# Seven block products in two units of five of a streamed fp32 down projection

## The chip, the core and the metric

One core of a Trainium2 chip runs the whole program. The metric is the time of one execution on the device in microseconds (us), as the median of several runs. Engines are named as the profile names them: PE (TensorE's matmuls), PEld (its weight loads), DVE (VectorE), ACT (ScalarE), POOL (GpSimd) and SP (the DMA queue that streams the weights).

## The reference

One layer of a hybrid block for 256 tokens and a model width of 2048, all in float32: a mixing part (gated MLP and windowed attention), then a gated MLP with a convolution of width 3. The change touches only the last matrix product.

```
def conv_ffn(h, w_up, conv_w, w_down):      # h (256, 2048), w_up (2048, 16384), w_down (8192, 2048)
    up = h @ w_up
    ...
    gate, val = conv[..., :D_FF], conv[..., D_FF:]
    return (jax.nn.gelu(gate, approximate=True) * val) @ w_down
...
x = x + rms_norm(conv_ffn(h2, w_up, conv_w, w_down), ln_post_ffn)
```

## The kernel before

**Splitting.** PE multiplies fp32r operands. To keep float32 accuracy each operand is held as a rounded part ("hi", written by ACT as a copy into an fp32r tile) and the rest ("lo", written by DVE as full minus hi), and each product is made as hi*hi + hi*lo + lo*hi, three matmuls. So every weight that comes from memory passes through ACT, then DVE, before PE may use it.

**The down projection.** `ffT` holds the 8192 hidden values of 256 tokens, transposed: 64 tiles of 128 hidden values by 256 tokens. Two sweeps each make 1024 of the 2048 output columns. A sweep reads the weights in 32 units of 1 MB (2 tiles of 128 hidden rows by 1024 columns) into the four slots of `raw`. A unit is two halves, each 128 hidden rows by 1024 columns. An ordinary half goes through a ring of four places in `w_hi`, `w_lo` and `xs`, and costs PE 2 token tiles x 3 parts x 2 column blocks = 12 matmuls of 512 columns (`half_b`, L1528); a unit costs 24.

**Units of seven products.** A unit is also a 2 x 2 by 2 x 2 block product: two tiles of hidden values, two tiles of 128 tokens, two blocks of 512 columns. For one unit in three of a sweep's middle the kernel makes it from seven block products instead of eight (Strassen's scheme in Winograd's form): 7 x 3 = 21 matmuls (`seven_products`, L1782 is the matmul's line). Its operands are not in the ring but in one set of buffers, the "forms": `b_hi`, `b_lo`, `s_hi`, `s_lo` (all inside `actT`) and `a_hi`, `a_lo` (`a_parts`). There is one set, so it must not be overwritten before PE has finished the seven products that read it. For such a unit ACT and DVE do this:

- `sum_forms` (DVE): seven sums and differences of the weight and activation blocks, in float32.
- `round_given` (ACT) and `rest_of_given` (DVE): hi and lo of the blocks that are used as they are.
- `round_sums` (ACT) and `rest_of_sums` (DVE): hi and lo of the sums.

Four of the seven products accumulate in four extra banks of PSUM; after the last such unit of a sweep `copy_p1` and `sum_products` make the terms that these banks still owe to the outputs, and in sweep 1 `round_u`, `rest_of_u` and `add_products` add them back with eight matmuls by an identity matrix.

**Counters.** Each engine runs its own list of instructions in order, and a wait holds all that stands behind it on that engine. `half_used` counts the halves that PE has finished since the kernel's start (a unit of seven products adds 2 at its end); `N_DOWN` is its value when the down projection begins. `hi_ready` and `lo_ready` count halves on ACT and DVE in the same numbering, `form_hi`, `form_lo` and `form_summed` count steps on the forms. `before` is the value of `half_used` at which all units ahead of a given place are done: before the change that place is the start of a group of three units, of which the third has the seven products. The wait in front of the first instruction that writes the forms is this one, in `round_given`:

```
act.wait_ge(half_used, gr.before - (4 if gr.first else 0))
```

SP refills a slot of `raw` when `lo_ready` says that DVE has read its unit.

Of the kernel before, what the change touches and what calls it, by code (L numbers as in the profile page):

```python
# [18 lines left out]
ALU = mybir.AluOpType  # L19
ACT = mybir.ActivationFunctionType  # L20
AX = mybir.AxisListType
F32 = mybir.dt.float32
# [52 lines left out]
def block_program(nc, x, x_t, pre_gains, w_in, ln_v_g, ln_v_b, w_spatial, b_spatial, rel_bias, sinks, w_a_out, w_b_out,  # L75
# [10 lines left out]
    with ExitStack() as ctx:  # L86
# [89 lines left out]

        def part_of_actT(k):
            return actT[:, k:k + 2, :, :].rearrange("p k a s -> p (k a s)")
# [240 lines left out]
        def _(act):  # L419
# [315 lines left out]
            def round_given(gr):  # L735

                block = raw[:, gr.slots[2], :]
                act.wait_ge(raw_landed[gr.slots[2]], gr.landed[2])
                act.wait_ge(half_used, gr.before - (4 if gr.first else 0))
                act.activation(b_hi[:, B2:BT], block[:, 2 * BLK:4 * BLK], ACT.Copy).then_inc(form_hi, 1)  # L740
                act.activation(b_hi[:, B1:B2], block[:, 0:BLK], ACT.Copy).then_inc(form_hi, 1)
                act.activation(a_hi[:, 0:S], ffT[:, gr.k + 5, :], ACT.Copy).then_inc(form_hi, 1)
                act.activation(a_hi[:, S:S + P], ffT[:, gr.k + 4, 0:P], ACT.Copy).then_inc(form_hi, 1)

            def round_sums(sweep, gr):

                n = SUMS * gr.forms
# [3 lines left out]
                act.activation(s_hi[:, 0:3 * P], s123, ACT.Copy).then_inc(form_hi, 1)  # L751
# [4 lines left out]
            def down_group(sweep, gr):  # L756

                for j in range(4):
                    if gr.first and j == 2:
                        round_given(gr)  # L760
                    act.wait_ge(half_used, gr.freed + j)
                    act.activation(xs[:, j, 0, :], ffT[:, gr.k + j, :], ACT.Copy)  # L762
                    slot = gr.slots[j // 2]
                    act.wait_ge(raw_landed[slot], gr.landed[j // 2])
                    act.activation(w_hi[:, j, :], raw[:, slot, j % 2 * HALF:(j % 2 + 1) * HALF], ACT.Copy).then_inc(hi_ready, 1)  # L765
                if not gr.first:
                    round_given(gr)
                round_sums(sweep, gr)

            def copy_p1(sweep, used):  # L770

                act.wait_ge(half_used, used)
                act.activation(yn[sweep][:, 0, 0:BLK], ps[:, 4 * sweep, :], ACT.Copy).then_inc(u_copied, 1)
# [8 lines left out]
            def down_turn(sweep, i, first=False, last=False):  # L782
# [3 lines left out]
                for h in range(LEFT if last and sweep == 0 else 0, 8):  # L786
                    if first and sweep == 1 and h == 2:
                        copy_p1(0, 8 * m - 2)
                    if first and sweep == 1 and h < 2:
                        free = h - 7  # L790
                    elif first and sweep == 1 and h < RING:
                        free = h - 3
                    elif last and sweep == 0:
                        free = h - 3
                    elif last and h < RING:
                        free = FREED[h]
                    else:
                        free = None
                    split_xs(m, h, ffT[:, 8 * i + h, :], free=free)
# [7 lines left out]
                    if last and sweep == 1 and h == 3:  # L807
                        copy_p1(1, 8 * m)
                        round_u()
# [5 lines left out]
            for sweep in range(2):  # L815
# [3 lines left out]
                for g in range(GROUPS[sweep]):  # L819
                    down_group(sweep, Group(sweep, g))  # L820
# [12 lines left out]
        def _(dve):  # L833
# [465 lines left out]
            def sum_forms(sweep, gr):  # L1299

                n = SUMS * gr.forms
                block = raw[:, gr.slots[2], :]
# [3 lines left out]
                a11, a21 = ffT[:, gr.k + 4, 0:P], ffT[:, gr.k + 4, P:S]  # L1306
                a12, a22 = ffT[:, gr.k + 5, 0:P], ffT[:, gr.k + 5, P:S]
# [15 lines left out]
            def rest(lo, full, hi):  # L1323
                dve.tensor_tensor(lo, full, hi.bitcast(F32), ALU.subtract).then_inc(form_lo, 1)

            def rest_of_given(gr):

                n = HALVES_HI * gr.forms
# [528 lines left out]
```

## Time and profile before

| | |
|---|---|
| median of 3 runs | 1600.2 us (1600.09 to 1600.46) |
| the profiled execution: its own time | 1600.68 us |
| the profiled execution: span of its instructions | 1598.9 us |
| mean granted TensorE clock | 0.999 of full speed |
| PE busy | 1589.9 us (99%) |
| DVE busy, whole span | 1221.4 us (76%) |
| ACT busy, whole span | 821.1 us (51%) |
| units of seven products | 17 (9 in sweep 0, 8 in sweep 1) |

The time of an execution is its span and a little around it: 1600.68 - 1598.9 = 1.8 us here. Busy times of PE are modelled, since matmuls overlap: a matmul's row says how long it is under way, and what it costs in a dense stream is the distance from its start to the next one's start.

### The profile page before, as it was taken

How to read it: one execution, taken by the hardware profiler on the slowest of the kernel's cores; microseconds unless marked ns; L12 is line 12 of the kernel's file. 1: busy time of each engine (PE TensorE's matmuls, PEld its weight loads, DVE VectorE, ACT ScalarE, POOL GpSimd, SP SyncE). 2: the span in 40 equal slices, each digit the busy share in tenths (PEclk: the TensorE clock that was granted, in tenths of full speed). 3: DMA queues.
4: the chain of work that ended last, by engine and by line, in shares of the span. 5: the costliest groups of instructions: out<-in, count | busy, mean ns of one | idle time of the engine just before them, and what ended most of it. 6: DMA issues, size and time to landing. Idle time of an engine off the chain costs nothing.

```text
span 1598.9 us, 24334 instructions
## 1 busy us (share of the span) xinstructions
PE 1589.9 (99%) x8673; PEld 1377.3 (86%) x8673; DVE 1221.4 (76%) x1777; ACT 821.1 (51%) x1119; POOL 2.0 (0%) x12
## 2 busy tenths in 40 slices
PE   9999999999999999999999999999999999999998
PEld 8888888888888888888888888888888888888886
DVE  6556677677766787777777777777777899979996
ACT  6544544456555654444444444444444656566663
POOL 0000000000000000000000000000000000000000
PEclk9999999999999999999999999999999999999999
DMA  9885455546565465656556565565655565546552
GB/s 369 268 230 185 159 184 171 171 158 210 193 255 193 149 210 184 192 184 200 185 184 190 185 200 186 184 189 185 200 186 184 210 232 190 210 160 235 203 192 79
DMA packets 234947, 313.17 MB, mean 196 GB/s; under 512 B 5360, under 2 KB 209808, under 8 KB 234000
## 3 DMA queue, kind: packets, MB, share of 16 engines
q1 hardware_dynamic: 231056, 306.44, 58.2%
q10 hardware_dynamic: 3840, 6.05, 1.5%
q8 instruction: 33, 0.54, 0.1%
q14 instruction: 18, 0.15, 0.0%
HBM read 309.58 MB, written 2.88 MB: 195 GB/s over the span
## 4 chain that ended last, share of the span: by engine, by line
PE 99%; DVE 0%; ACT 0%; issue 0%; DVEq 0%
PE ps L1445 44%; PE ps L1449 23%; PE ps L1536 20%; PE ps L1782 5%; PE ps L1584 3%; PE ps L1549 1%; PE ps L1460 1%; PE ps L1465 0%; PE ps L1673 0%; PE ps L1654 0%; PE ps L1606 0%; PE ps L1666 0%; PE ps L1683 0%; PE ps L1731 0%; DVE arena L1421 0%; PE ps L1489 0%
## 5 line engine op out<-in xcount | busy, mean ns | idle before, releaser
L837 DVE TENSOR_TENSOR w_lo<-raw,w_hi 128x1024 fp32r<-128x1024 f32 x464 | 557.4, 1222 | 243.3 <-ACT w_hi L428 240.4
L428 ACT ACTIVATE w_hi<-raw 128x1024 fp32r<-128x1024 f32 x462 | 478.0, 1057 | 513.3 <-PE ps L1445 261.1
L1445 PE MATMUL ps<-actT,w_hi 128*128 128x512 f32 x3072 | 717.1, 390 | 0.0
L1445 PEld LDWEIGHTS ps<-actT,w_hi 128*128 128x128 f32 x3072 | 569.9, 188 | 114.1 <-issue 0.2
L1449 PEld LDWEIGHTS ps<-actT,w_lo 128*128 128x128 f32 x3072 | 383.4, 191 | 10.0 <-issue 1.7
L1449 PE MATMUL ps<-actT,w_lo 128*128 128x256 f32 x3072 | 389.4, 283 | 0.0
L1536 PE MATMUL ps<-w_hi,xs 128*128 128x512 f32 x944 | 255.4, 389 | 0.0
L1536 PEld LDWEIGHTS ps<-w_hi,xs 128*128 128x128 f32 x944 | 177.2, 188 | 36.7
L1536 PE MATMUL ps<-w_lo,xs 128*128 128x512 f32 x472 | 145.3, 389 | 0.0
L1249 DVE SCALAR_TENSOR_TENSOR arena<-arena,convw 128x256 f32<-128x256 f32 x256 | 106.8, 480 | 0.1
L1536 PEld LDWEIGHTS ps<-w_lo,xs 128*128 128x128 f32 x472 | 88.6, 188 | 18.4
L1359 DVE TENSOR_TENSOR w_lo<-raw,w_hi 128x1024 fp32r<-128x1024 f32 x68 | 83.4, 1226 | 0.0
L848 DVE TENSOR_TENSOR arena<-ps,arena 128x512 f32<-128x512 f32 (+1 forms) x106 | 72.6, 685 | 1.6 <-ACT arena L441 1.6
L765 ACT ACTIVATE w_hi<-raw 128x1024 fp32r<-128x1024 f32 x68 | 71.2, 1047 | 0.0
L441 ACT ACTIVATE arena<-ps 128x512 f32<-128x512 f32 x106 | 61.4, 580 | 2.9 <-PE ps L1465 1.4
L1782 PE MATMUL ps<-actT 128*128 128x512 f32 x204 | 57.7, 391 | 0.0
L843 DVE TENSOR_TENSOR xs<-arena,xs 128x256 fp32r<-128x256 f32 x58 | 24.6, 423 | 43.1 <-ACT w_hi L428 42.8
L434 ACT ACTIVATE xs<-arena 128x256 fp32r<-128x256 f32 x58 | 24.0, 414 | 61.9 <-PE ps L1536 50.8
L762 ACT ACTIVATE xs<-arena 128x256 fp32r<-128x256 f32 x68 | 27.9, 410 | 43.4 <-PE ps L1536 43.4
L1237 DVE TENSOR_TENSOR arena<-arena,rrow 128x512 f32<-128x512 f32 x64 | 44.3, 693 | 6.5
L1782 PE MATMUL ps<-actT,a_parts 128*128 128x512 f32 x153 | 46.7, 395 | 0.0
L1245 DVE TENSOR_SCALAR arena<-arena,convw 128x256 f32<-128x256 f32 x128 | 39.5, 351 | 8.9 <-DVE arena L1237 0.2
(176 smaller groups left out, 881.4 us busy)
## 6 DMA issues: line engine op xcount, KB each, us to landing
raw<-in_w_up_dram SPq DMA_DIRECT2D x128, 1024.0 KB, 5.8
raw<-in_w_down_dram SPq DMA_DIRECT2D x64, 1024.0 KB, 5.2
raw<-in_w_in_dram SPq DMA_DIRECT2D x58, 1024.0 KB, 5.2
raw<-in_w_o_dram SPq DMA_DIRECT2D x16, 1024.0 KB, 5.2
raw<-in_w_a_out_dram SPq DMA_DIRECT2D x8, 1024.0 KB, 5.5
raw<-in_w_b_out_dram SPq DMA_DIRECT2D x8, 1024.0 KB, 5.5
arena<-in_x_dram SPq DMA_DIRECT2D x1, 2048.0 KB, 17.1
arena<-in_x_dram ACTq DMA_DIRECT2D x2, 1024.0 KB, 6.6
```

Of the source, the lines that this page charges most:

```text
L428: act.activation(w_hi[:, h % RING, :], raw[:, h // 2, h % 2 * HALF:(h % 2 + 1) * HALF], ACT.Copy)\
L441: act.activation(lo_part, ps[:, bank:bank + 2, S:2 * S], ACT.Copy).then_inc(copied, 1)
L765: act.activation(w_hi[:, j, :], raw[:, slot, j % 2 * HALF:(j % 2 + 1) * HALF], ACT.Copy).then_inc(hi_ready, 1)
L837: dve.tensor_tensor(w_lo[:, h % RING, :], raw[:, h // 2, h % 2 * HALF:(h % 2 + 1) * HALF], w_hi[:, h % RING, :].bitcast(F32), ALU.subtract ...
L848: dve.tensor_tensor(dst, ps[:, bank:bank + 2, 0:S], lo_part, ALU.add).then_inc(summed, 1)
L1249: dve.scalar_tensor_tensor(out=dst[:, a, :], in0=src[:, a, i:i + S], scalar=w(i, a), in1=dst[:, a, :], op0=ALU.mult, op1=ALU.add).then_inc ...
L1359: dve.tensor_tensor(w_lo[:, j, :], raw[:, gr.slots[j // 2], j % 2 * HALF:(j % 2 + 1) * HALF], w_hi[:, j, :].bitcast(F32), ALU.subtract).th ...
L1445: return pe.matmul(ps[:, bank + c, :], w_hi[:, h % RING, at:at + P], actT[:, k, :, :].rearrange("p a s -> p (a s)"), start=start, stop=stop)
L1449: return pe.matmul(ps[:, bank + c, 0:S], w_lo[:, h % RING, at:at + P], actT[:, k, 0, :], start=start, stop=stop)
L1536: ins = pe.matmul(ps[:, bank + 2 * t + c, :], xpart[:, tokens], wpart[:, slot, c * 512:(c + 1) * 512], start=(first and xpart is x_hi and ...
L1584: ins = pe.matmul(ps[:, 4 + 2 * t + c, :], xpart[:, t * P:(t + 1) * P], wpart[:, slot, c * 512:(c + 1) * 512], start=(k == 0 and xpart is ...
L1782: ins = pe.matmul(ps[:, bank, :], x[x_part], y[y_part], start=(first and alone and x_part + y_part == 0), stop=(last and alone and x_part ...
```

## The change

In a sweep's middle 25 units now form five groups of five, and the third and the fifth unit of each (`s1`, `s2`) have seven products: 20 in both sweeps instead of 17. The two token tiles change places in the scheme, so that the given activation blocks lie side by side and one instruction (128x384) converts them where there were two (128x256 and 128x128). PE waits three times at such a unit: for the given blocks (`form_lo` + 3), for the sums' first part (`form_lo` + 5), and for all (`lo_ready`). A class `Unit` takes the place of `Group`: its `before` belongs to the unit itself. Three units (halves 2 to 7 of the last turn) are left at a sweep's end, and the work of `copy_p1`, `sum_products`, `round_u`, `rest_of_u` and `add_products` is placed between those halves.

```diff
-        SUMS, HALVES_HI = 7, 7
-        FREED = (-5, -4, -3, -2)
-        GROUPS = ((FF // P // 2 - RAW) // 3, (FF // P // 2 - 2 * RAW) // 3)
-        LEFT = (RAW + 3 * GROUPS[0]) * 2 - (FF // P - 8)
-
-        class Group:
-
-
-            def __init__(self, sweep, g):
-                unit = RAW + 3 * g
-                self.k = 2 * unit
-                self.before = N_DOWN + FF // P * sweep + 2 * unit
-                self.freed = self.before - (3 if g == 0 else 5)
-                self.slots = [(unit + x) % RAW for x in range(3)]
-                self.landed = [16 * ((self.before // 2 + x) // RAW + 1) for x in range(3)]
-                self.forms = GROUPS[0] * sweep + g
-                self.first = g == 0
+        SUMS, HALVES_HI = 7, 5
+        GROUPS = 5
+        SEVENS = [RAW + 5 * g + x for g in range(GROUPS) for x in (2, 4)]
+        LEFT = 2 * (RAW + 5 * GROUPS) - (FF // P - 8)
+        DONE = [N_DOWN + FF // P * sweep + 2 * u + j + 1
+                for sweep in range(2) for u in range(FF // P // 2) if u not in SEVENS for j in range(2)]
+
+        class Unit:
+
+
+            def __init__(self, sweep, u):
+                self.k = 2 * u
+                self.before = N_DOWN + FF // P * sweep + 2 * u
+                self.slot = u % RAW
+                self.landed = 16 * (self.before // 2 // RAW + 1)
+                sevens = [x for x in SEVENS if x < u]
+                self.forms = len(SEVENS) * sweep + len(sevens)
+                self.place = (FF // P - 2 * len(SEVENS)) * sweep + 2 * (u - len(sevens))
+                self.first = u == SEVENS[0]
+                self.last = u == SEVENS[-1]
+
+        SEVENS_DONE = [Unit(sweep, SEVENS[-1]).before + 2 for sweep in range(2)]
+
+        def free_at(sweep, h):
+
+            place = Unit(sweep, h // 2).place + h % 2
+            return DONE[place - RING] if place >= RING else N_DOWN + place - RING + 1
...
-            def round_given(gr):
-
-                block = raw[:, gr.slots[2], :]
-                act.wait_ge(raw_landed[gr.slots[2]], gr.landed[2])
-                act.wait_ge(half_used, gr.before - (4 if gr.first else 0))
+            def round_given(unit):
+
+                block = raw[:, unit.slot, :]
+                act.wait_ge(raw_landed[unit.slot], unit.landed)
+                act.wait_ge(half_used, unit.before - (4 if unit.first else 0))
                 act.activation(b_hi[:, B2:BT], block[:, 2 * BLK:4 * BLK], ACT.Copy).then_inc(form_hi, 1)
                 act.activation(b_hi[:, B1:B2], block[:, 0:BLK], ACT.Copy).then_inc(form_hi, 1)
-                act.activation(a_hi[:, 0:S], ffT[:, gr.k + 5, :], ACT.Copy).then_inc(form_hi, 1)
-                act.activation(a_hi[:, S:S + P], ffT[:, gr.k + 4, 0:P], ACT.Copy).then_inc(form_hi, 1)
-
-            def round_sums(sweep, gr):
-
-                n = SUMS * gr.forms
+                act.activation(a_hi, given(unit), ACT.Copy).then_inc(form_hi, 1)
+
+            def round_sums(sweep, unit):
+
+                n = SUMS * unit.forms
                 act.wait_ge(form_summed, n + 2)
                 act.activation(b_hi[:, BT:BT + 2 * BLK], yn[sweep][:, 0, :], ACT.Copy).then_inc(form_hi, 1)
                 act.wait_ge(form_summed, n + 6)
-                act.activation(s_hi[:, 0:3 * P], s123, ACT.Copy).then_inc(form_hi, 1)
+                act.activation(s_hi[:, 0:3 * P], s123, ACT.Copy)
                 act.activation(s_hi[:, 3 * P:4 * P], s4, ACT.Copy).then_inc(form_hi, 1)
                 act.wait_ge(form_summed, n + 7)
                 act.activation(b_hi[:, BT + 2 * BLK:BT + 4 * BLK], yn[sweep][:, 1, :], ACT.Copy).then_inc(hi_ready, 2)
 
-            def down_group(sweep, gr):
-
-                for j in range(4):
-                    if gr.first and j == 2:
-                        round_given(gr)
-                    act.wait_ge(half_used, gr.freed + j)
-                    act.activation(xs[:, j, 0, :], ffT[:, gr.k + j, :], ACT.Copy)
-                    slot = gr.slots[j // 2]
-                    act.wait_ge(raw_landed[slot], gr.landed[j // 2])
-                    act.activation(w_hi[:, j, :], raw[:, slot, j % 2 * HALF:(j % 2 + 1) * HALF], ACT.Copy).then_inc(hi_ready, 1)
-                if not gr.first:
-                    round_given(gr)
-                round_sums(sweep, gr)
+            def down_unit(sweep, unit):
+
+                for j in range(2):
+                    slot = (unit.place + j) % RING
+                    act.wait_ge(half_used, free_at(sweep, unit.k + j))
+                    act.activation(xs[:, slot, 0, :], ffT[:, unit.k + j, :], ACT.Copy)
+                    act.wait_ge(raw_landed[unit.slot], unit.landed)
+                    act.activation(w_hi[:, slot, :], raw[:, unit.slot, j * HALF:(j + 1) * HALF], ACT.Copy).then_inc(hi_ready, 1)
+
+            def down_group(sweep, g):
+
+                o1, o2, s1, o3, s2 = (Unit(sweep, RAW + 5 * g + x) for x in range(5))
+                down_unit(sweep, o1)
+                if s1.first:
+                    round_given(s1)
+                    down_unit(sweep, o2)
+                else:
+                    down_unit(sweep, o2)
+                    round_given(s1)
+                round_sums(sweep, s1)
+                down_unit(sweep, o3)
+                round_given(s2)
+                round_sums(sweep, s2)
...
+                for h in range(LEFT if last else 0, 8):
+                    if last and h == 6:
+                        copy_p1(sweep, SEVENS_DONE[sweep])
+                    split_xs(m, h, ffT[:, 8 * i + h, :], free=free_at(sweep, 8 * i + h) - 8 * m)
+                    if last and sweep == 1 and h == 6:
+                        round_u()
...
-                dve.wait_ge(lo_ready, gr.before + 2)
-                dve.wait_ge(raw_landed[gr.slots[2]], gr.landed[2])
+                dve.wait_ge(lo_ready, unit.before - 2)
+                dve.wait_ge(raw_landed[unit.slot], unit.landed)
...
+            def rest_of_given(unit):
+
+                n = HALVES_HI * unit.forms
                 dve.wait_ge(form_hi, n + 1)
-                rest(b_lo[:, B2:BT], raw[:, gr.slots[2], 2 * BLK:4 * BLK], b_hi[:, B2:BT])
+                rest(b_lo[:, B2:BT], raw[:, unit.slot, 2 * BLK:4 * BLK], b_hi[:, B2:BT]).then_inc(form_lo, 1)
                 dve.wait_ge(form_hi, n + 2)
-                rest(b_lo[:, B1:B2], raw[:, gr.slots[2], 0:BLK], b_hi[:, B1:B2])
+                rest(b_lo[:, B1:B2], raw[:, unit.slot, 0:BLK], b_hi[:, B1:B2]).then_inc(form_lo, 1)
                 dve.wait_ge(form_hi, n + 3)
-                rest(a_lo[:, 0:S], ffT[:, gr.k + 5, :], a_hi[:, 0:S])
+                rest(a_lo, given(unit), a_hi).then_inc(form_lo, 1)
...
+            def down_group(sweep, g):
+
+                o1, o2, s1, o3, s2 = (Unit(sweep, RAW + 5 * g + x) for x in range(5))
+                down_unit(sweep, o1)
+                sum_forms(sweep, s1)
+                if s1.first:
+                    rest_of_given(s1)
+                    down_unit(sweep, o2)
+                else:
+                    down_unit(sweep, o2)
+                    rest_of_given(s1)
+                rest_of_sums(sweep, s1)
+                down_unit(sweep, o3)
+                sum_forms(sweep, s2)
+                rest_of_given(s2)
+                rest_of_sums(sweep, s2)
 
...
+                    if products and h == 7:
+                        products()
...
-                pe.wait_ge(lo_ready, ready)
-                for side_by_side in ((p1, p2), (p3, p4), (p5, p6, p7)):
-                    for x_part, y_part in ((0, 0), (0, 1), (1, 0)):
-                        for x, y, bank, alone in side_by_side:
-                            ins = pe.matmul(ps[:, bank, :], x[x_part], y[y_part],
-                                            start=(first and alone and x_part + y_part == 0),
-                                            stop=(last and alone and x_part == 1))
-                ins.then_inc(half_used, 2)
+                pe.wait_ge(form_lo, HALVES_HI * unit.forms + 3)
+                together((p1, p2))
+                pe.wait_ge(form_lo, HALVES_HI * unit.forms + 5)
+                together((p3, p5, p7))
+                pe.wait_ge(lo_ready, unit.before + 2)
+                together((p4, p6)).then_inc(half_used, 2)
...
-                for g in range(GROUPS[sweep]):
-                    gr = Group(sweep, g)
-                    for j in range(4):
-                        half_b(gr.before + j + 1, j, bank, False, False)
-                    seven_products(gr.before + 6, bank, p_bank, gr.first, g == GROUPS[sweep] - 1)
-                b_turn(m + turns - 1, bank, range(LEFT, 8) if sweep == 0 else range(4), last=True)
-            add_products()
-            last_halves(N_END // 8 - 1)
+                for u in range(RAW, RAW + 5 * GROUPS):
+                    unit = Unit(sweep, u)
+                    if u in SEVENS:
+                        seven_products(unit, bank, p_bank)
+                    else:
+                        for j in range(2):
+                            half_b(unit.before + j + 1, (unit.place + j) % RING, bank, False, False)
+                b_turn(m + turns - 1, bank, range(LEFT, 8) if sweep == 0 else range(LEFT, 4), last=True)
+            last_halves(N_END // 8 - 1, products=add_products)
```

ACT, in the middle of the down projection, before: two ordinary units (`xs`, `w_hi`) and then the forms of the third (writes into `actT` and `a_parts`).

```order
L762 ACTIVATE xs<-arena 128x256 [waits half_used]
L765 ACTIVATE w_hi<-raw 128x1024 [waits raw_landed0]
L762 ACTIVATE xs<-arena 128x256 [waits half_used]
L765 ACTIVATE w_hi<-raw 128x1024 [waits raw_landed0]
L740 ACTIVATE actT<-raw 128x1024 [waits half_used,raw_landed1]
L741 ACTIVATE actT<-raw 128x512
L742 ACTIVATE a_parts<-arena 128x256
L743 ACTIVATE a_parts<-arena 128x128
L749 ACTIVATE actT<-arena 128x1024 [waits form_summed]
L751 ACTIVATE actT<-convw 128x384 [waits form_summed]
L752 ACTIVATE actT<-rrow 128x128
L754 ACTIVATE actT<-arena 128x1024 [waits form_summed]
```

ACT at the same kind of place after the change: the unit `o3` and the forms of `s2`.

```order
L775 ACTIVATE xs<-arena 128x256 [waits half_used]
L777 ACTIVATE w_hi<-raw 128x1024 [waits raw_landed3]
L775 ACTIVATE xs<-arena 128x256 [waits half_used]
L777 ACTIVATE w_hi<-raw 128x1024 [waits raw_landed3]
L755 ACTIVATE actT<-raw 128x1024 [waits half_used,raw_landed0]
L756 ACTIVATE actT<-raw 128x512
L757 ACTIVATE a_parts<-arena 128x384
L763 ACTIVATE actT<-arena 128x1024 [waits form_summed]
L765 ACTIVATE actT<-convw 128x384 [waits form_summed]
L766 ACTIVATE actT<-rrow 128x128
L768 ACTIVATE actT<-arena 128x1024 [waits form_summed]
```

The order of the conversions has stayed, with one instruction less; the wait on `half_used` in front of the first of them is still there, with another value: in the diff it is the own `before` of the unit with seven products, where it was that of the group, four halves lower.

PE at a unit of seven products, before:

```order
L1536 MATMUL ps<-w_hi,xs 128x512 x2
L1782 MATMUL ps<-actT,a_parts 128x512 [waits lo_ready]
L1782 MATMUL ps<-actT,a_parts 128x512 x5
L1782 MATMUL ps<-actT 128x512
L1782 MATMUL ps<-actT,a_parts 128x512
```

PE at such a unit after the change:

```order
L1555 MATMUL ps<-w_hi,xs 128x512 x2
L1795 MATMUL ps<-actT,a_parts 128x512 [waits form_lo]
L1795 MATMUL ps<-actT,a_parts 128x512 x5
L1795 MATMUL ps<-actT 128x512 [waits form_lo]
L1795 MATMUL ps<-actT 128x512 x8
L1795 MATMUL ps<-actT,a_parts 128x512 [waits lo_ready]
```

The 21 matmuls are now in three parts of 6, 9 and 6, each behind a wait of its own; the products p3, p5 and p7 stand in the middle, and p4 and p6, which need the last converted sum, at the end.

## Rows read from the trace of the kernel before

**Rows 1.** The page: span, busy time and share of each engine.

```profile
span 1598.9 us, 24334 instructions
PE 1589.9 (99%) x8673; PEld 1377.3 (86%) x8673; DVE 1221.4 (76%) x1777; ACT 821.1 (51%) x1119; POOL 2.0 (0%) x12
```

**Rows 2.** Waits of the whole span: us in total, times, longest us.

```profile
PE ps L1606 <- DVE rrow L905: 1.2, 1, 1.2
PE ps L1723 <- DVE arena L1165: 0.5, 1, 0.5
...
ACT actT L740 <- PE ps L1782: 53.0, 15, 3.5
```

**Rows 3.** Windows of three groups (PE, PEld, DVE, ACT, POOL busy; clock; DMA).

```profile
1304.90:1320.70 15.80, 15.80 (x71) 13.04 (x70) 14.51 (x25) 9.85 (x16) 0.00 (x0) 1.00 0.56 202
1320.70:1336.40 15.70, 15.70 (x71) 12.94 (x70) 14.41 (x24) 9.86 (x16) 0.00 (x0) 1.00 0.55 202
```

**Rows 4.** Timeline of ACT from one unit's forms to the next group's.

```profile
1305.54 1.06 ACT L740 ACTIVATE actT<-raw 128x1024 fp32r<-128x1024 f32 x1 [3.53 <-PE ps L1782]
...
1309.10 1.05 ACT L754 ACTIVATE actT<-arena 128x1024 fp32r<-128x1024 f32 x1
1310.06 0.40 ACT L762 ACTIVATE xs<-arena 128x256 fp32r<-128x256 f32 x1
1310.36 1.04 ACT L765 ACTIVATE w_hi<-raw 128x1024 fp32r<-128x1024 f32 x1
1311.31 0.40 ACT L762 ACTIVATE xs<-arena 128x256 fp32r<-128x256 f32 x1
...
1321.26 1.06 ACT L740 ACTIVATE actT<-raw 128x1024 fp32r<-128x1024 f32 x1 [3.53 <-PE ps L1782]
```

**Rows 5.** Timeline of DVE: sums, forms and the next ordinary half.

```profile
1303.52 0.28 DVE L1311 TENSOR_TENSOR convw<-arena 128x128 f32<-128x128 f32 x1
...
1306.67 1.82 DVE L1324 TENSOR_TENSOR actT<-raw,actT 128x1024 fp32r<-128x1024 f32 x2
1308.41 0.62 DVE L1324 TENSOR_TENSOR a_parts<-arena,a_parts 128x256 fp32r<-128x256 f32 x2
1308.94 1.22 DVE L1324 TENSOR_TENSOR actT<-arena,actT 128x1024 fp32r<-128x1024 f32 x1
1310.08 0.56 DVE L1324 TENSOR_TENSOR actT<-convw,actT 128x384 fp32r<-128x384 f32 x1
1310.55 0.29 DVE L1324 TENSOR_TENSOR actT<-rrow,actT 128x128 fp32r<-128x128 f32 x1
1310.75 1.22 DVE L1348 TENSOR_TENSOR actT<-arena,actT 128x1024 fp32r<-128x1024 f32 x1
1311.88 0.43 DVE L1358 TENSOR_TENSOR xs<-arena,xs 128x256 fp32r<-128x256 f32 x1
...
1313.35 0.42 DVE L1358 TENSOR_TENSOR xs<-arena,xs 128x256 fp32r<-128x256 f32 x1
```

**Rows 6.** Timeline of PE around a unit of seven products and its successor.

```profile
1300.44 1.56 PE L1782 MATMUL ps<-actT,a_parts 128*128 128x512 f32 x6
...
1305.29 0.62 PE L1536 MATMUL ps<-w_hi,xs 128*128 128x512 f32 x2
...
1316.16 1.56 PE L1782 MATMUL ps<-actT,a_parts 128*128 128x512 f32 x6
```

**Rows 7.** Timeline where PE waits for DVE, after the output projection.

```profile
532.43 0.75 DVE L1165 SCALAR_TENSOR_TENSOR arena<-arena,stat 128x512 f32<-128x512 f32 x1
...
533.35 0.59 PEld L1723 LDWEIGHTS ps<-ident,arena 128*128 128x128 f32 x4
...
533.58 0.60 PE L1723 MATMUL ps<-ident,arena 128*128 128x128 f32 x4
```

**Rows 8.** The last matmul, then windows after it (clock is third from last).

```profile
1591.63 0.39 PE L1549 MATMUL ps<-w_hi,xs 128*128 128x512 f32 x1
...
1594.00:1594.10 0.10, 0.00 (x0) 0.00 (x0) 0.10 (x1) 0.00 (x0) 0.00 (x0) 1.00 0.94 369
1594.10:1594.20 0.10, 0.00 (x0) 0.00 (x0) 0.10 (x1) 0.00 (x0) 0.00 (x0) 0.58 0.06 0
1594.20:1594.30 0.10, 0.00 (x0) 0.00 (x0) 0.10 (x1) 0.00 (x0) 0.00 (x0) 0.50 0.02 0
```

**Rows 9.** Timeline of PE's first matmuls.

```profile
1.20 0.58 PE L1606 MATMUL ps<-rrow 128*128 128x128 f32 x1 [1.20 <-DVE rrow L905]
...
6.01 1.05 PE L1584 MATMUL ps<-w_hi,actT 128*128 128x512 f32 x2
6.44 0.85 PE L1584 MATMUL ps<-w_hi,actT 128*128 128x512 f32 x2
8.05 1.09 PE L1584 MATMUL ps<-w_lo,actT 128*128 128x512 f32 x4
```

More of the change, by code:

```diff
@@ L175, in block_program, with given @@
         gain2 = region(22528, D)
+        def given(unit):
+            return ffT[:, unit.k:unit.k + 2, :].rearrange("p k s -> p (k s)")[:, P:4 * P]
         def part_of_actT(k):
@@ L818, in _ @@
                     down_turn(1, 0, first=True)
-                for g in range(GROUPS[sweep]):
-                    down_group(sweep, Group(sweep, g))
+                for g in range(GROUPS):
+                    down_group(sweep, g)
                 down_turn(sweep, turns - 1, last=True)
@@ L1296, in _, with sum_forms @@
                 up_turn(it)
-            def sum_forms(sweep, gr):
-                n = SUMS * gr.forms
-                block = raw[:, gr.slots[2], :]
+            def sum_forms(sweep, unit):
+                n = SUMS * unit.forms
+                block = raw[:, unit.slot, :]
                 quarters = block.rearrange("p (a b c) -> p a b c", a=2, b=2)
@@ new lines, in rest_of_sums, with down_unit @@
+                rest(s_lo[:, 3 * P:4 * P], s4, s_hi[:, 3 * P:4 * P]).then_inc(form_lo, 1)
+                dve.wait_ge(hi_ready, unit.before + 2)
+                rest(b_lo[:, BT + 2 * BLK:BT + 4 * BLK], yn[sweep][:, 1, :], b_hi[:, BT + 2 * BLK:BT + 4 * BLK])\
+                    .then_inc(lo_ready, 2)
+            def down_unit(sweep, unit):
+                for j in range(2):
+                    slot = (unit.place + j) % RING
+                    dve.wait_ge(hi_ready, unit.before + j + 1)
+                    rest(xs[:, slot, 1, :], ffT[:, unit.k + j, :], xs[:, slot, 0, :])
+                    rest(w_lo[:, slot, :], raw[:, unit.slot, j * HALF:(j + 1) * HALF], w_hi[:, slot, :]).then_inc(lo_ready, 1)
@@ L1385, in down_turn @@
                 m = i + (N_DOWN // 8 + sweep * (FF // P // 8))
-                for h in range(LEFT if last and sweep == 0 else 0, 8):
-                    if first and sweep == 1 and h == 2:
-                        sum_products(0)
+                for h in range(LEFT if last else 0, 8):
+                    if last and h == 6:
+                        sum_products(sweep)
                     split_xs(m, h, ffT[:, 8 * i + h, :])
+                    if last and sweep == 1 and h == 6:
+                        rest_of_u()
                     if first and sweep == 0 and h == 3:
@@ L1403, in down_turn @@
                             dve.tensor_tensor(yn[0][:, t, :], yn[0][:, t, :], gain2[:, 0:SW], ALU.mult).then_inc(sw_out, 1)
-                    if last and sweep == 1 and h == 3:
-                        sum_products(1)
-                        rest_of_u()
             turns = FF // P // 8
@@ L1413, in _ @@
                     down_turn(1, 0, first=True)
-                for g in range(GROUPS[sweep]):
-                    down_group(sweep, Group(sweep, g))
+                for g in range(GROUPS):
+                    down_group(sweep, g)
                 down_turn(sweep, turns - 1, last=True)
@@ L1758, in _, with seven_products, a_given @@
             turns = FF // P // 8
-            def seven_products(ready, c_bank, p_bank, first=False, last=False):
-                def a_given(at):
-                    return a_hi[:, at:at + P], a_lo[:, at:at + P]
+            def seven_products(unit, c_bank, p_bank):
+                def a_given(q):
+                    return a_hi[:, q * P:(q + 1) * P], a_lo[:, q * P:(q + 1) * P]
                 def a_sum(q):
@@ L1769, in b, with together @@
                     return b_hi[:, at:at + BLK], b_lo[:, at:at + BLK]
-                p1 = (a_given(S), b(B1), p_bank, True)
-                p2 = (a_given(0), b(B2), c_bank, False)
-                p3 = (a_sum(3), b(B2 + BLK), c_bank + 1, False)
-                p4 = (a_given(P), b(BT + 3 * BLK), c_bank + 2, False)
+                def together(products):
+                    for x_part, y_part in ((0, 0), (0, 1), (1, 0)):
+                        for x, y, bank, alone in products:
+                            ins = pe.matmul(ps[:, bank, :], x[x_part], y[y_part],
+                                            start=(unit.first and alone and x_part + y_part == 0),
+                                            stop=(unit.last and alone and x_part == 1))
+                    return ins
+                p1 = (a_given(0), b(B1), p_bank, True)
+                p2 = (a_given(2), b(B2), c_bank + 2, False)
+                p3 = (a_sum(3), b(B2 + BLK), c_bank + 3, False)
+                p4 = (a_given(1), b(BT + 3 * BLK), c_bank, False)
                 p5 = (a_sum(0), b(BT), p_bank + 1, True)
```

65 lines of the change are left out of this document (13 added, 52 removed).

## The prediction

> **What bounds the kernel now.** The page's shares come first: PE is busy 99% of the span, DVE 76%, ACT 51% [rows 1]. The list of waits then says whether something hides behind that: PE's two longest waits are 1.2 us at the start and 0.5 us in the middle, none of them in the down projection [rows 2]. So PE's stream of matmuls is the time, and what a change does is what it takes out of that stream and what holes it makes in it. Third, the windows over the groups of three: PE is busy for all of 15.70 us, DVE for 14.41, ACT for 9.86 [rows 3]. DVE is near its limit, so I read its timeline too. A group of three starts its seven products at 1300.44 and the next at 1316.16 [rows 6]: 15.72 us for 24 + 24 + 21 = 69 matmuls, 0.228 us each. That is a matmul's price; an ordinary half is 2.73 us, a unit 5.47, one of seven products 4.78.
>
> The fourth reading decides the case. ACT sits idle 3.53 us before the first conversion of the forms and is released by the end of the previous seven products (15 times, 53.0 us in all) [rows 2, 4]. It costs nothing: PE starts the next ordinary unit at 1305.29, ACT the forms at 1305.54, 0.25 us later, DVE ends them at 1310.75 + 1.22 = 1311.97, and PE wants them at 1316.16, 4.2 us later [rows 4 to 6]. Two ordinary units, 10.9 us of matmuls, cover the conversion.
>
> **Fewer matmuls.** 20 units of seven instead of 17: 3 x 3 = 9 matmuls fewer, -2.05 us. The eight identity matmuls stay.
>
> **The forms' wait, moved by four halves.** The new wait asks `half_used` for the unit's own `before`, and that value is reached only when PE has finished the unit directly ahead. PE's next instructions are the seven products, whose operands ACT may only now begin to convert. The cover is gone: PE must sit out the chain. Queued behind ACT's wait are this unit's roundings and the next ordinary unit's; DVE waits for the first, PE for DVE. Take A as the start of ACT's first conversion, 0.25 us after the moment when PE's next matmul would have started [rows 4, 6].
>
> - Given blocks. In the rows DVE's first rest starts 1306.67 - 1305.54 = 1.13 after A, its two instructions last until the start of the activations' rest at A + 2.87 (1308.41) [rows 4, 5]. That is one 128x384 instruction now; the 128x384 of the sums has 0.56 us [rows 5]. End: A + 3.43.
> - From DVE's end to the matmul. The one place where PE waits for such an end: DVE ends at 532.43 + 0.75 = 533.18, the weight load starts at 533.35, the matmul at 533.58 [rows 7]; 0.40 us.
> - First hole: 0.25 + 3.43 + 0.40 = 4.08 us.
> - Second wait. From the 384's start the next starts 0.47 later (1310.08 to 1310.55), so DVE starts the first sums' rest (1024) at A + 3.34; from there to the end of the 128 it takes 1310.55 + 0.29 - 1308.94 = 1.90 [rows 5]: A + 5.24, PE at A + 5.64. PE's six matmuls began at A + 3.83 and last 1.37, until A + 5.20: a second hole of 0.44 us.
> - Third wait. DVE's last rest ends 1311.97 - 1308.94 = 3.03 after A + 3.34, at A + 6.37; the nine matmuls last until A + 7.69. No hole.
> - The next ordinary unit. DVE turns to it at A + 6.28 and needs 1313.35 - 1311.88 = 1.47 a half [rows 5]: first half ready near A + 7.8, PE is through at A + 9.06. ACT has it earlier (0.96 after its last form, 1.25 a half) [rows 4]. Covered, by 1 us.
>
> So 4.5 us a unit. Which ones? The first of each sweep has 4 less in its wait: it is released when the first turn ends, with `o1` and `o2` (10.9 us) to cover it. The other 18 have it: 18 x 4.52 = +81.4 us. Could the sums add to it? DVE makes them before the hole, while PE works: after `s2` it has `o1` (2.94), the sums (1306.67 - 1303.52 = 3.15) and half of `o2`, up to about A + 13.9, where PE asks for `o2` at A + 14.5. That is 0.6 us of cover, and the tightest of the ordinary places.
>
> **The other edits.** One instruction less on ACT and on DVE per such unit saves some 0.06 us of the chain (counted above). The three waits instead of one are worth something only in a hole: with a single wait PE would start at A + 6.77 instead of A + 3.83, so they save up to 2.5 us of it (counted above). At the end of sweep 1 the last seven products finish at A + 9.06, the eight identity matmuls are due four ordinary halves' worth (two whole halves and the first token tile of three, 9.6 us) later, and the copies, sums and rests fit on ACT and DVE with about nothing over: 0 to 0.5 us, I take 0.3. The tail after the last matmul is the same list.
>
> **TensorE's clock.** The granted clock stood at 1.00 until 1594.10 and at 0.50 from 1594.20, 2.1 us after the last matmul's end (1591.63 + 0.39) [rows 8]: the lower level, 1.2 GHz. The holes will be about 3.9 us without a matmul, longer than that. So I expect it to fall at most of them. What low clock costs: PE's matmuls of 512 columns at the very start begin 0.43 us apart (6.01, 6.44), twice 0.228 less a little, and from about 6.87 they go at the full rate, 5.7 us after PE's first at 1.20 [rows 9]. Each matmul at the lower level is thus 0.20 us late. How long it stays low after a hole no row shows: between nothing and those 5.7 us (13 matmuls, 2.7 us). I take two thirds, 3.8 us, because part of the low stretch may lie inside the hole: 9 matmuls, 1.8 us, less the second hole, which slower matmuls fill: +1.36 a unit, +24.5 us over 18.
>
> The Trainium skill, "TensorE: Matmul & The Clock Gate", says in "HAM oscillation" that a loop which leaves the engine idle between bursts pays the return to the slow clock at every burst. By that page the cold start-to-start of a 512-column matmul is 426.7 ns, an estimate of 0.20 us lost for each, and the same sum as from the rows; the tail's fall agrees with it, and no row of this case shows a fall between two bursts.
>
> **Sum.** The profiled execution is 1600.68 us, 0.5 over the median, which I take as base: 1600.2 - 2.05 + 81.4 + 0.3 = 1679.9, and with the clock's 24.5 about 1704 us.
>
> **The rivals.**
>
> - *The clock holds.* Only a fall after the end of all work is on record, not one in a hole. Then 1679.9 us. Chance 0.22.
> - *The clock stays low longer*, 5.7 us or more after each hole: (2.7 - 0.44) x 18 = 41, 1721 us, and up to 1760 if the ordinary units suffer too. 0.10.
> - *Not slower: the wait is met in time.* If ACT came to the forms when PE's counter had long passed, or if the count awaited were two halves (5.5 us) lower than I read it, the 4.5 us of chain would be covered, and the time would be 1598.2, within 0.2%. For it: three of the new waits are of the kind that start PE early. Against: the same wait, four halves lower, already holds ACT 3.5 us each time [rows 2], so ACT is ahead of PE, not behind. 0.04.
> - *DVE becomes the bound.* Per five units it would need 3 x 2.94 + 2 x 8.30 = 25.4 us (8.36 from 1303.52 to 1311.88, less 0.06) against PE's 114 x 0.228 = 26.0. With the holes a group lasts 35 us or more and DVE has air; without them this would be the next limit, at 1598 to 1602 us. It shares the previous case's chance: 0.02.
>
> **How the numbers follow.** The forecast, falls of the clock at most holes, has the remaining 0.62 and gives 1690 to 1720. With the clock steady the time is near 1680 (1676 if the release lag of 0.40 is 0.17 less), and the bound of 5.7 us gives 1721; the range 1675 to 1726 leaves out the long stay's upper part and the two cases without holes, some 0.13. A measurement of this kernel tells about 0.2% from no change. Slower by over 0.2%: 0.94; within: 0.05; faster: 0.01.
>
> **What the changed kernel's profile would show.** PE's matmul line of the seven products has waits of about 4 us, 18 times, released by DVE's activations' rest, and 18 smaller ones (0.4 us or none); ACT's first conversion is released by an ordinary half's matmul instead of by the seven products; 420 matmuls of seven products; DVE's share in the groups falls from 92% to about 70%; windows of a few us behind the holes have a granted clock between 0.5 and 1. Wrong would be: no such waits (then the count was misread), a clock of 1.00 all through (then 1680), or waits released by something other than the given blocks' chain, the ordinary unit `o2` above all.

## The result, and the profile after

| | before | after |
|---|---|---|
| median | 1600.26 us (6 runs, 1600.09 to 1600.88) | 1704.89 us (6 runs, 1699.1 to 1706.01) |
| ratio (of the means) | | 1.0645, 95% interval 1.0628 to 1.0661 |
| span of the profiled execution | 1598.9 us | 1702.8 us |
| mean granted clock | 0.999 | 0.972 |

The change costs 104.6 us. The page of the kernel after it, to be read against [rows 1]; its third line is the group of matmuls that open a unit of seven products, the last ACT's first conversion for the forms:

```profile
span 1702.8 us, 24335 instructions
PE 1630.1 (96%) x8664; PEld 1400.8 (82%) x8664; DVE 1236.4 (73%) x1790; ACT 821.4 (48%) x1111; POOL 2.0 (0%) x12
...
L1795 PE MATMUL ps<-actT,a_parts 128*128 128x512 f32 x180 | 75.6, 526 | 63.6 <-DVE a_parts L1337 63.6
...
L755 ACT ACTIVATE actT<-raw 128x1024 fp32r<-128x1024 f32 x20 | 21.1, 1057 | 200.8 <-PE ps L1555 200.8
```

PE has the 9 matmuls fewer (8673 to 8664) and 64 us of idleness in front of that group; a matmul of it is under way for 526 ns on average, where it was 395 before. And ACT waits 200.8 us in front of its first conversion, released by an ordinary half (L1555) where it was the seven products (L1782) in [rows 2]. The lists of waits of PE and ACT (us in total, times, longest):

```profile
PE ps L1795 <- DVE a_parts L1337: 63.6, 18, 3.5
PE ps L1627 <- DVE rrow L918: 1.2, 1, 1.2
PE ps L1744 <- DVE arena L1178: 0.5, 1, 0.5
...
ACT actT L755 <- PE ps L1555: 200.8, 20, 12.9
```

Eighteen waits, as counted from the diff. The timeline of one of them, an `s1`:

```profile
1331.02 0.61 PE L1555 MATMUL ps<-w_hi,xs 128*128 128x512 f32 x2
1331.73 1.06 ACT L755 ACTIVATE actT<-raw 128x1024 fp32r<-128x1024 f32 x1 [9.67 <-PE ps L1555]
...
1332.82 1.83 DVE L1337 TENSOR_TENSOR actT<-raw,actT 128x1024 fp32r<-128x1024 f32 x2 [5.35 <-ACT actT L755]
...
1334.56 0.55 DVE L1337 TENSOR_TENSOR a_parts<-arena,a_parts 128x384 fp32r<-128x384 f32 x1
...
1335.17 2.21 PEld L1795 LDWEIGHTS ps<-actT,a_parts 128*128 128x128 f32 x6 [3.96 <-DVE a_parts L1337]
1335.17 2.93 PE L1795 MATMUL ps<-actT,a_parts 128*128 128x512 f32 x6 [3.54 <-DVE a_parts L1337]
...
1337.90 3.75 PE L1795 MATMUL ps<-actT 128*128 128x512 f32 x9
...
1342.88 0.62 PE L1555 MATMUL ps<-w_hi,xs 128*128 128x512 f32 x2
```

The reader is to see three engines, one at a time. PE's last ordinary matmul starts at 1331.25, so the next one would be due at 1331.48. ACT begins at 1331.73, DVE ends the last given block at 1334.56 + 0.55 = 1335.11, and PE is back at 1335.17: a hole of 3.69 us. (The list says 3.5, because a matmul's modelled end lies 0.16 us behind the moment when the next one could start.) Then the six first matmuls take 2.73 us instead of 1.40, and the whole unit 1342.88 - 1335.17 = 7.71 instead of the 4.85 of the kernel before (1300.44 to 1305.29 in [rows 6]). The windows of the hole, of the seven products and of the two ordinary units behind them (the clock is third from last):

```profile
1331.50:1335.10 3.60, 0.13 (x1) 0.00 (x0) 2.28 (x4) 3.37 (x6) 0.00 (x0) 0.90 0.00 0
1335.17:1342.88 7.71, 7.71 (x21) 6.12 (x22) 7.68 (x13) 6.07 (x10) 0.00 (x0) 0.61 0.42 143
1342.88:1353.80 10.92, 10.92 (x49) 8.82 (x47) 4.33 (x7) 0.00 (x0) 0.00 (x0) 1.00 0.51 189
```

The clock has fallen to its lower level near the hole's end (0.90 on average in it) and is there for most of the seven products (0.61), where matmuls start 0.427 us apart; the two ordinary units behind run at full speed. Over the 18 units behind a hole the trace gives 7.02 us each on average, 2.17 more than 4.85.

### The profile page after: what moved, and what is told of

It is laid out like the page before. It is cut to its first block, busy times and chain, and to the rows that moved or that the text cites. A ratio compares the mean times of both kernels' runs of the same rounds, so it can differ in the third digit from the quotient of the medians.

```text
span 1702.8 us, 24335 instructions
## 1 busy us (share of the span) xinstructions
PE 1630.1 (96%) x8664; PEld 1400.8 (82%) x8664; DVE 1236.4 (73%) x1790; ACT 821.4 (48%) x1111; POOL 2.0 (0%) x12
## 4 chain that ended last, share of the span: by engine, by line
PE 96%; DVE 3%; ACT 1%; issue 0%; DVEq 0%; ACTq 0%
PE ps L1464 41%; PE ps L1468 22%; PE ps L1555 18%; PE ps L1795 8%; PE ps L1605 3%; DVE actT L1337 2%; PE ps L1568 1%; ACT actT L755 1%; PE ps L1479 1%; DVE a_parts L1337 1%; PE ps L1484 0%; PE ps L1694 0%; PE ps L1675 0%; PE ps L1627 0%; PE ps L1687 0%
## 5 line engine op out<-in xcount | busy, mean ns | idle before, releaser
L850 DVE TENSOR_TENSOR w_lo<-raw,w_hi 128x1024 fp32r<-128x1024 f32 x466 | 559.8, 1222 | 242.7 <-ACT w_hi L443 239.9
L1555 PE MATMUL ps<-w_hi,xs 128*128 128x512 f32 x896 | 243.2, 389 | 0.0
L1555 PEld LDWEIGHTS ps<-w_hi,xs 128*128 128x128 f32 x896 | 168.1, 188 | 35.1
L1555 PE MATMUL ps<-w_lo,xs 128*128 128x512 f32 x448 | 137.9, 389 | 0.0
L1795 PE MATMUL ps<-actT,a_parts 128*128 128x512 f32 x180 | 75.6, 526 | 63.6 <-DVE a_parts L1337 63.6
L755 ACT ACTIVATE actT<-raw 128x1024 fp32r<-128x1024 f32 x20 | 21.1, 1057 | 200.8 <-PE ps L1555 200.8
L1337 DVE TENSOR_TENSOR actT<-raw,actT 128x1024 fp32r<-128x1024 f32 (+1 forms) x40 | 36.5, 955 | 110.1 <-ACT actT L755 110.1
L1795 PEld LDWEIGHTS ps<-actT,a_parts 128*128 128x128 f32 x180 | 43.5, 252 | 80.7 <-DVE a_parts L1337 71.2
L1555 PEld LDWEIGHTS ps<-w_lo,xs 128*128 128x128 f32 x448 | 84.1, 188 | 17.5
L1795 PE MATMUL ps<-actT 128*128 128x512 f32 x240 | 86.8, 483 | 0.1
L1795 PEld LDWEIGHTS ps<-actT 128*128 128x128 f32 x240 | 60.9, 254 | 17.5 <-DVE actT L1337 1.1
L1337 DVE TENSOR_TENSOR w_lo<-raw,w_hi 128x1024 fp32r<-128x1024 f32 x60 | 73.2, 1220 | 0.0
L856 DVE TENSOR_TENSOR xs<-arena,xs 128x256 fp32r<-128x256 f32 x60 | 25.4, 423 | 41.4 <-ACT w_hi L443 41.3
```

The lines of the kernel that those rows point to most:

```text
L850: dve.tensor_tensor(w_lo[:, h % RING, :], raw[:, h // 2, h % 2 * HALF:(h % 2 + 1) * HALF], w_hi[:, h % RING, :].bitcast(F32), ALU.subtract ...
L1337: return dve.tensor_tensor(lo, full, hi.bitcast(F32), ALU.subtract)
L1555: ins = pe.matmul(ps[:, bank + 2 * t + c, :], xpart[:, tokens], wpart[:, slot, c * 512:(c + 1) * 512], start=(first and xpart is x_hi and ...
L1795: ins = pe.matmul(ps[:, bank, :], x[x_part], y[y_part], start=(unit.first and alone and x_part + y_part == 0), stop=(unit.last and alone a ...
```

## The experiments

**The wait at the previous seven products.** The forms are free when the previous seven products are done: four halves below the unit's own `before` for s1, two for s2.

```diff
-                act.wait_ge(half_used, unit.before - (4 if unit.first else 0))
+                act.wait_ge(half_used, unit.before - (4 if (unit.k // 2 - RAW) % 5 == 2 else 2))
```

> The changed kernel with one edit: the wait ahead of the forms asks for the end of the previous seven products (the unit's before less 4 for s1, less 2 for s2) instead of the end of the unit directly ahead. Theory (the chain of conversions stands uncovered because the wait is met too late, and the holes cool the clock): no hole is left, since s2 has one ordinary unit (5.47 us) over the 3.7 us of chain and s1 two; 9 matmuls fewer than in the kernel before, 1598.2 us, clock 0.999. Rival (DVE is the bound, 25.4 of 26.0 us in five units, and the later wait only shows it): waits of PE for ordinary halves or for the sums appear, 1602 to 1615 us.

Measured: 1598.98 us (11 runs), ratio to the kernel before 0.999 (0.9981 to 0.9999), clock 0.999. PE has no wait in the down projection. Windows in its groups:

```profile
1310.00:1360.00 50.00, 50.00 (x221) 41.09 (x219) 49.10 (x78) 33.10 (x52) 0.00 (x0) 1.00 0.55 197
1360.00:1410.00 50.00, 50.00 (x220) 41.12 (x219) 48.94 (x76) 28.72 (x46) 0.00 (x0) 1.00 0.60 219
```

PE is busy for all of it, DVE for 98%, and it still hides. The whole loss of 106 us hangs on this one value; the rest of the change gains 1.57 us on the kernel before, which took 1600.55 us beside it (2.05 expected). It is the fastest version of this study.

**One half of cover.** The same wait at `unit.before - 1`.

```diff
-                act.wait_ge(half_used, unit.before - (4 if unit.first else 0))
+                act.wait_ge(half_used, unit.before - (4 if unit.first else 1))
```

> The changed kernel with the wait one half lower (before less 1, all units but the first of a sweep): one ordinary half, 2.73 us, covers part of the chain. Theory: the first hole is 3.70 - 2.73 = 0.97 us, the second (for the sums' first part) stays at about 0.5, and holes as short as that leave the clock alone: 18 x 1.47 = 26 us over 1598.2, so 1625 us, clock 0.999. Rival (each hole costs a fixed amount for the clock's fall, however short): 18 x 2.2 us more, 1660 us.

Measured: 1626.53 us, clock 0.999. The list of waits:

```profile
PE ps L1795 <- DVE a_parts L1337: 14.8, 18, 0.8
...
PE ps L1795 <- DVE actT L1337: 0.3, 2, 0.2
```

27.6 us over the version above, 1.53 a unit where 1.47 was expected: what the chain lacks in cover, and no clock. The hole ahead of the unit is 0.98 us in the timeline, and the unit itself takes 5.37 us instead of 4.85. A fixed price per hole is out.

**The hole filled.** At the 18 units PE runs 14 small matmuls by zeros ahead of the wait (zeros are added to an output bank; the profile shows each of these fp32 matmuls as two instructions).

```diff
+                if not unit.first:
+                    pe.wait_ge(zero_set, 1)
+                    for _ in range(14):
+                        pe.matmul(ps[0:64, c_bank, 0:P], zeros, ident[:], start=False, stop=False)
                 pe.wait_ge(form_lo, HALVES_HI * unit.forms + 3)
```

> The changed kernel, with 14 small matmuls by zeros (64x128 stationary, 128 columns in fp32) put ahead of the wait for the given blocks at the 18 units that wait; they add nothing to the sums and take about 3 us of the 3.7 at the full clock. Theory (a third of the loss is the clock): the holes stay, the clock does not fall, 1598.2 + 18 x (3.7 + 0.5) = 1674 us, clock 0.99 or more. Rival (the slow matmuls behind the holes have another cause than PE's idleness, such as DVE and ACT reading the same memory): 1705 us or more, since the zeros help nothing.

Measured: 1675.22 us, clock 0.999. In the timeline the same hole, filled:

```profile
1314.05 0.61 PE L1558 MATMUL ps<-w_hi,xs 128*128 128x512 f32 x2
1314.59 3.27 PE L1813 MATMUL ps<-ident,arena 128*64 128x128 f32 x28
1318.20 1.67 PE L1798 MATMUL ps<-actT,a_parts 128*128 128x512 f32 x6 [0.33 <-DVE a_parts L1339]
1320.00 2.35 PE L1798 MATMUL ps<-actT 128*128 128x512 f32 x9
...
1323.59 0.62 PE L1558 MATMUL ps<-w_hi,xs 128*128 128x512 f32 x2
```

The seven products start no earlier (1314.51 to 1318.20, 3.69 us), but they run at the full rate, and the kernel is 29.7 us faster with more work for PE. So the slow matmuls behind the holes came from PE's idleness, 29.7 / 18 = 1.65 us a unit. The rest, 1675.22 - 1598.98 = 76.2 or 4.24 a unit, is 3.69 of hole and 0.55: the unit takes 5.39 us here (1318.20 to 1323.59; 5.37 on average) instead of 4.85. The starts of its single matmuls show two parts of that. Before the nine at 1320.00 lies a gap of 0.30 us, the second wait; and after each of the two waits the second matmul starts 0.33 us behind the first instead of 0.23, so that each restart costs 0.10.

With 7 of them instead of 14 an idle piece is left:

> As the filled kernel, with 7 small matmuls instead of 14: they take about 1.6 us of the 3.7, and 2.1 us stay idle in one piece. Theory (the clock falls for idleness, and less often for a shorter piece): between 1674 and 1690 us. Rival (any idle piece over 2 us brings the whole fall, as after the last matmul): 1700 to 1705 us.

Measured: 1681.53 us (1680.82 to 1684.19), PE's waits:

```profile
PE ps L1798 <- DVE a_parts L1339: 33.5, 18, 1.9
```

Windows of its two sweeps have a granted clock of 0.99 and 0.97. The clock still falls at 4 of the 18 holes: these four units take 6.54 to 6.81 us, the other fourteen 5.36 to 5.39. That is 6.3 us in all. In the changed kernel it falls at 17 of 18. So pieces of 1.9 us idle, with small matmuls in the rest of the hole, bring it down far less often than holes that are idle throughout.

**One kind of unit alone.** The wait lowered for s1 only (before less 4), and for s2 only (before less 2).

> The wait lowered for s1 alone (before less 4), left for s2. Ten units (five of each sweep) keep the wait for the unit directly ahead. Theory (each such unit costs the same, hole and clock, 5.9 us as measured between this kernel's two ends): 1599.0 + 10 x 5.9 = 1658 us, give or take 5 for where the clock's falls lie. Rival (the first hole of a group starves what follows, so the loss is per group): 1599 + 53 = 1652 for one per group whichever it is, the same as for s2 alone.

> The wait lowered for s2 alone (before less 2), left for s1, of which the first of a sweep has none. Eight units keep it. Theory: 1599.0 + 8 x 5.9 = 1646 us, 12 below s1 alone. Rival (loss per group): the same as s1 alone.

Measured: 1655.87 and 1644.90 us. The first line is of s1 alone, the second of s2 alone:

```profile
PE ps L1795 <- DVE a_parts L1337: 35.4, 10, 3.5
```

```profile
PE ps L1795 <- DVE a_parts L1337: 28.3, 8, 3.5
```

5.69 us for each of ten, 5.74 for each of eight: the loss belongs to the unit, and the two add up to 56.9 + 45.9 = 102.8 of 105.9; the 3.1 that are left lie within the 7 us by which runs of the changed kernel differ.

**The kernel before with the wait moved**, and nothing else:

```diff
-                act.wait_ge(half_used, gr.before - (4 if gr.first else 0))
+                act.wait_ge(half_used, gr.before + (0 if gr.first else 4))
```

> The kernel before with only the wait moved: the group's before plus 4 (all but the first unit of a sweep), groups of three, 17 units of seven, one wait of PE for all the forms. Theory (the moved wait is the whole loss, whatever the groups): 15 holes of 0.25 + 6.4 + 0.1 = 6.7 us, 100 us, and 1 to 2.3 us for the clock at each: 1716 to 1735 us, most likely 1728. Rival (the loss comes of two units in five and DVE's load): 1600 to 1610 us.

Measured: 1724.83 us, ratio 1.078 (1.0764 to 1.0797), clock 0.969.

```profile
PE ps L1782 <- DVE actT L1348: 98.1, 15, 6.5
```

124.3 us over the kernel before in the same job, 8.3 us for each of 15 units: 6.7 of hole (6.54 on average in the list, and the 0.16 of the modelled end) and 1.6 for the slower matmuls and the restart behind it. That is more than the changed kernel loses, with fewer units, since its one wait makes PE sit out the whole chain. The loss does not need the groups of five.

**One wait instead of three**, in the changed kernel and in the version with the wait at the previous seven products:

```diff
-                pe.wait_ge(form_lo, HALVES_HI * unit.forms + 3)
+                pe.wait_ge(lo_ready, unit.before + 2)
                 together((p1, p2))
-                pe.wait_ge(form_lo, HALVES_HI * unit.forms + 5)
                 together((p3, p5, p7))
-                pe.wait_ge(lo_ready, unit.before + 2)
                 together((p4, p6)).then_inc(half_used, 2)
```

> The changed kernel with one wait of PE for all the forms in place of three. Theory (the hole ends when the last piece that PE waits for is there): the hole becomes 0.25 + 6.37 + 0.06 = 6.7 us and costs 8.3 us with the clock, as in the kernel before with the wait moved: 1599 + 18 x 8.3 = 1748 us. Rival (DVE's and ACT's chain is what paces the group, whenever PE starts): 1705 us.

> The kernel with the wait at the end of the previous seven products (1599.0 us) with one wait of PE for all the forms. Theory: s1 has two units of cover and does not care; s2 has 5.47 us of cover for 6.7 us of chain, so ten holes of 1.2 us: 1611 us, clock 0.999. Rival (three waits are worth nothing where the chain is covered): 1599 us.

Measured: 1761.55 and 1611.91 us. The first line is of the changed kernel with one wait, the second of the other:

```profile
PE ps L1795 <- DVE actT L1337: 116.6, 18, 6.5
```

```profile
PE ps L1795 <- DVE actT L1337: 10.3, 10, 1.0
```

So the three waits are worth 56.7 us where the chain stands bare (1748 was expected: 163 us over 1599 is 9.0 a unit, 6.6 of hole and 2.4 behind it instead of the 1.6 of the kernel before with the wait moved; why more, no run shows), and 12.9 us where s2 has one unit of cover. Without them two units of five would be no gain: 1611.91 us is 11.4 over the kernel before.

**DVE's air.** In the version with the wait at the previous seven products, one conversion is made twice.

```diff
-                rest(b_lo[:, BT:BT + 2 * BLK], yn[sweep][:, 0, :], b_hi[:, BT:BT + 2 * BLK]).then_inc(form_lo, 1)
+                rest(b_lo[:, BT:BT + 2 * BLK], yn[sweep][:, 0, :], b_hi[:, BT:BT + 2 * BLK]).then_inc(again, 1)
+                dve.wait_ge(again, unit.forms + 1)
+                rest(b_lo[:, BT:BT + 2 * BLK], yn[sweep][:, 0, :], b_hi[:, BT:BT + 2 * BLK]).then_inc(form_lo, 1)
```

> The kernel with the wait at the end of the previous seven products, with one conversion of DVE (128x1024) made twice at each unit of seven, the second behind the first's end (about 1.25 us more). DVE's work in five units goes from 25.3 to 27.8 us against PE's 26.0. Theory (DVE is the next limit, 0.7 us of air in five units): ten groups become some 1.8 us longer, 1599 + 18 = 1617 us, and PE waits for DVE. Rival (PE's cover takes it): 1599 to 1602 us.

Measured: 1615.63 us, 16.7 over 1598.98, 1.67 a group. Its windows over the groups:

```profile
1310.00:1360.00 50.00, 47.08 (x202) 37.42 (x201) 49.83 (x78) 30.46 (x48) 0.00 (x0) 1.00 0.52 190
1360.00:1410.00 50.00, 47.12 (x203) 37.45 (x202) 49.83 (x74) 29.05 (x46) 0.00 (x0) 1.00 0.48 173
```

DVE is now busy all the time and PE 94%, and PE waits for DVE's conversion of the sums eight times:

```profile
PE ps L1798 <- DVE actT L1338: 11.2, 8, 1.4
```

These are the `s2` of every group but the first of a sweep. Such a group takes 28.06 us (1310.26 to 1338.32) instead of 26.04, the first one only 26.10. The bound has changed hands.

## Why the prediction was right

The path, the releaser, the count of 18 and the fall of the clock came out as predicted. The sum's terms were less exact than its total, which owes much of its closeness to errors that cancelled.

- **The matmuls taken out**, -2.05 us: 1.57 measured. The price of 0.228 is a mean over two kinds. In [rows 6] the seven products take 4.85 us (1300.44 to 1305.29), 0.231 a matmul, and the two ordinary units behind them 10.87 (1305.29 to 1316.16), 5.44 a unit and not 5.47. So a unit that changes over saves 0.59 us, and three save 1.8; [rows 6] already showed it.
- **The cover gone, 18 times**: 18 waits with the predicted releaser; each kind of unit alone brings its share, the old kernel with only this value moved brings the loss too, and the value moved back takes all of it away. Shown.
- **First hole**, 4.08 us: 3.69 measured. ACT started 0.25 after PE's due time, as predicted, and DVE ended at A + 3.38 (3.43 predicted). The mis-sized part is the step from DVE's end to PE's matmul, 0.40 by [rows 7]: after the long wait weight load and matmul both started 0.06 us after DVE's end. The reading of [rows 7] was wrong, for PE did not stand still there. The matmul ahead of the one at 533.58 started at 533.35, the usual 0.23 earlier, so DVE's end at 533.18 held nothing up, and the 0.40 is only an upper bound:

```profile
533.35 0.39 PE L1549 MATMUL ps<-w_hi,xs 128*128 128x512 f32 x1
```

- **Second hole**, 0.44 us: 0.30 at full clock in the filled kernel. What the sum lacks are the two restarts of PE, 0.10 each. First hole, second hole and restarts make 4.19 of the 4.24 a unit that the filled kernel loses (4.52 predicted). **Third wait**, none: none in the list.
- **The clock**, +1.36 a unit: 1.65 measured, shown by the filled kernel. The price of a slow matmul was right: they start 0.427 us apart, 0.20 more than at full clock. The low stretch under work was 4.5 us on average over the 18 units, where I had chosen 3.8 between 0 and 5.7; this choice was not worked out from rows of a fall between bursts, and it came out too low.
- **Luck.** The holes' error and the clock's cancelled (-0.28 x 18 = -5, +0.29 x 18 = +5). So did those of the matmuls taken out and of the end of sweep 1 (+0.3 and -0.3). By parts: 4.52 + 1.36 = 5.88 a unit predicted, 4.24 + 1.65 = 5.89 measured. That 1704 meets 1704.89 so closely is owed to this, and the runs themselves lie between 1699 and 1706.
- **The end of sweep 1**, +0.3: PE has no wait for the identity matmuls in the list of the changed kernel or of the version with the wait moved back; the term was too high.
- **DVE as a rival bound**: not here, but rightly priced; 25.4 of 26.0 us left 0.6, and 1.25 x 2 more made a full group 2.0 longer.
- **The clock holds** was the nearest rival. The filled kernel is what it would have been: 1675 against the 1680 that I gave it.
- What stays open: what exactly makes a given hole bring the clock down, and for how long. Of the 18 holes of 3.7 us in the trace the one at 1298.50 did not (first six matmuls in 1.81 us from start to start), and the next did (2.73). Of the units behind the other 17, seven take 6.3 to 6.5 us and ten 7.4 to 7.8. The runs of the changed kernel differ by 7 us, where the kernels without falls differ by under 1. The two shortest (1699.1 and 1700.8) have a mean granted clock of 0.977 and 0.976, the four others 0.971 or 0.972, so the difference goes with the clock; why it differs from run to run was not tried.

```profile
1298.50 1.66 PE L1795 MATMUL ps<-actT,a_parts 128*128 128x512 f32 x6 [3.54 <-DVE a_parts L1337]
1318.49 2.93 PE L1795 MATMUL ps<-actT,a_parts 128*128 128x512 f32 x6 [3.54 <-DVE a_parts L1337]
```

## What to carry to other kernels

When a counter's reference point changes its owner (a group's start became a unit's start), every offset that was written against it must be worked out again: ask of each wait which event frees the buffer, and how many microseconds of the waited-for engine's work lie between that event and the need. A wait that costs nothing, such as ACT's 53 us before, is a measure of how early the engine is; compare its cover with the chain behind it before moving it. And split the wait for a chain of conversions by what is needed first: it was worth 12.9 us in the good version, 56.7 in the bad one.

## What the runs showed of the hardware

- A hole of 3.7 us in front of dense matmuls brought the clock down 17 times of 18, and the lower level added 1.65 us a unit on average. PE can be kept at full rate with work that changes nothing (14 small matmuls by zeros, -29.7 us over 18 holes). Holes of 1.0 and 1.2 us did not bring the clock down at all (0.999).
- A unit of seven products takes 4.85 us in a dense stream. Behind holes of 3.7 us it took 2.17 more on average. Behind holes of 6.6 to 6.7 us it took 1.6 more in the kernel before with the wait moved and 2.4 in the changed one with one wait: the longer hole did not make the slow stretch behind it much dearer, since much of the low stretch lies inside the hole (3.6 us of it in the first, 3.0 in the second, on average).
- At the lower level matmuls of 512 columns start 0.427 us apart, at full clock 0.227 to 0.236 (ordinary units 0.2265, seven products 0.231 on average).
- After a long wait PE's weight load and matmul start together, 0.06 us after the releasing DVE instruction's end, and at full clock the second matmul follows 0.33 us later; in a dense stream the load leads by 0.23 us. So each restart costs 0.10 us beyond the hole (in the version with the wait at the previous seven products and one wait of PE, ten holes of 1.19 and ten restarts make 12.9 us).
- DVE busy for 49.1 of 50 us and PE for 50 of 50 at once left PE without one wait in the whole down projection.
